# TensorE's order in a recurrence, a strip copy moved ahead of a root, and a closing stage in token halves

## The reference, cut to what matters

```
u = shift(h @ w_in)                              # "strips": u = keep*p + mu_prev*prev + mu_next*next
c_q, c_kv = c_q / rms(c_q), c_kv / rms(c_kv)     # the roots of the attention latents
S = S*w_t - (S kk_t) b_t + v_t k_t ; y_t = S r_t # 8 heads, forward and backward over the tokens
z = ALPHA*h + [y_att, y_rwkv] @ w_out
h = (z - mean(z)) / sqrt(var(z) + eps) * ln1_g + ln1_b
logits = h @ router
```

## Time and profile before

| | us |
|---|---|
| median of 3 runs (3505.91 to 3512.84) | 3507.08 |
| profiled execution, its own time | 3508.14 |
| its span, first to last instruction | 3505.9 |
| TensorE busy in the span | 3055.5 (87%) |
| VectorE, ScalarE, GpSimd busy | 1765.5, 843.7, 573.7 |
| mean granted TensorE clock | 0.933 |
| recurrence stage, layer 1 and 2 (first to last matmul) | 357.5 to 611.5, 1378.2 to 1632 |
| first y slot to the end of line 1787, layer 1 | 663.52 to 723.88 |
| the same, layer 2 | 1684.13 to 1742.29 |

### The profile page before, as it was taken

The page is one execution under the profiler, slowest core; times in us unless marked ns, Lnnn a source line. Parts: engine busy times, 40 slices in busy tenths (PEclk is TensorE's granted clock), DMA queues, the critical chain, the costliest instruction groups (busy, mean ns, idle before and its releaser), DMA issues. The chain is left out here.

```text
span 3505.9 us, 67363 instructions
## 1 busy us (share of the span) xinstructions
PE 3055.5 (87%) x27902; PEld 2335.8 (67%) x27902; DVE 1765.5 (50%) x3348; ACT 843.7 (24%) x1768; POOL 573.7 (16%) x895
## 2 busy tenths in 40 slices
PE   6899898958767997899868769899998899999998
PEld 4676788735436775887644434576656688778887
DVE  3445576441123444676421145255467776577742
ACT  3123222031122223222211132233354211122210
POOL 0000674011110003672011110000055200000000
PEclk9998799979988997899979979999999999999999
DMA  7110300269984102102199982101010122222220
GB/s 248 41 37 28 146 4 4 84 256 380 403 298 133 42 19 115 62 4 87 37 367 389 403 252 97 38 25 43 20 37 13 60 73 96 82 67 93 81 90 33
DMA packets 171506, 419.71 MB, mean 120 GB/s; under 512 B 30113, under 2 KB 116513, under 8 KB 145745
## 3 DMA queue, kind: packets, MB, share of 16 engines
q1 hardware_dynamic: 152241, 381.49, 29.2%
q0 software_dynamic: 8736, 17.32, 2.0%
q10 hardware_dynamic: 10240, 16.79, 1.5%
HBM read 398.82 MB, written 50.54 MB: 128 GB/s over the span
## 5 line engine op out<-in xcount | busy, mean ns | idle before, releaser
L2181 PE MATMUL ps<-e_w,e_xt 128*64 128x256 f32 x1792 | 231.0, 415 | 71.5 <-DMA e_w<-in_moe_w 70.1
L2181 PEld LDWEIGHTS ps<-e_w,e_xt 128*64 128x64 f32 x1792 | 151.8, 150 | 172.3 <-issue 84.1
L775 PE MATMUL ps<-h,win 128*128 128x264 f32 x960 | 229.5, 393 | 16.4 <-DVE pad L944 14.8
L2288 DVE TENSOR_TENSOR e_hid<-ps,e_silu 64x256 f32<-64x256 f32 x64 | 39.4, 615 | 399.8 <-ACT e_silu L2247 399.8
L775 PEld LDWEIGHTS ps<-h,win 128*128 128x128 f32 x960 | 182.8, 193 | 53.0 <-issue 22.0
L1462 PE MATMUL ps<-inv,nt 48*48 48x48 f32 x4224 | 133.6, 211 | 2.3 <-issue 2.3
L3712 PE MATMUL ps<-h_lat,wt 128*128 128x256 f32 x528 | 127.8, 384 | 6.7 <-ACT h_lat L3849 6.5
L3712 PE MATMUL ps<-h_lat,w_sums 128*128 128x256 f32 x544 | 130.8, 384 | 0.0
L2200 PE MATMUL ps<-e_w,e_hid_t 128*64 128x512 f32 x448 | 111.6, 617 | 12.6 <-DMA e_w<-in_moe_w 7.9
L1462 PEld LDWEIGHTS ps<-inv,nt 48*48 48x48 f32 x4224 | 116.9, 127 | 5.3 <-issue 2.6
L3712 PEld LDWEIGHTS ps<-h_lat,wt 128*128 128x128 f32 x528 | 101.1, 192 | 23.2 <-issue 7.3
(11 more groups left out here) (671 smaller groups left out, 6928.4 us busy)
## 6 DMA issues: line engine op xcount, KB each, us to landing
e_w<-in_moe_w SPq DMA_DIRECT2D x168, 1024.0 KB, 13.6
early<-in_moe_w SPq DMA_DIRECT2D x24, 1024.0 KB, 13.1
wt<-in_w_up SPq DMA_DIRECT2D x22, 1024.0 KB, 4.9
y_rows<-e_y ACTq DMA_DIRECT2D x128, 128.0 KB
win<-in_w_in SPq DMA_DIRECT2D x10, 1536.0 KB, 6.7
wmod<-in_w_mod SPq DMA_DIRECT2D x24, 512.0 KB, 15.1
wt<-in_w_in SPq DMA_DIRECT2D x11, 1024.0 KB, 4.8
early<-in_w_mod SPq DMA_DIRECT2D x16, 512.0 KB, 10.7
```

The source lines that it names most:

```text
L775: last = pe.matmul(ps[:, 7, 0:HT], lhsT=ring[(s + 1) % 2][:, i, o:o + P], rhs=k.h[:, i, h * HT:(h + 1) * HT], start=(i == 0), stop=(i == K ...
L2181: last = pe.matmul(ps[half, 2 + z, 0:EH], lhsT=xt[z][:, f, :], rhs=w[:, f, :], start=(f == 0), stop=(f == KD - 1))
L2288: dve.tensor_tensor(hid[z][high, :].rearrange("s (t q) -> s q t", t=2), ps[high, 2 + z, 0:EH].rearrange("s (q t) -> s q t", t=2), si[z][hi ...
```

## The change

TensorE alone takes the recurrence in another order: in a step, a chain that is at its last phase comes behind the others (11, 7, 3, 15). The other engines keep `woven()` as it was. In `mix_in` VectorE does `empty(1)` ahead of root 1 and `empty(2)` ahead of root 2. In `mix_close` the y slots come per half (eight y0 for columns 0 to 263, then eight y1), GpSimd adds the first six tiles of a half (`fold`), and mean, squares, root, reciprocal and router are done for half 0 between the y1 slots, for half 1 behind them.

```diff
+                    if t == 1:
+                        pe.wait_ge(root, 2)
...
                 empty(0)
+                empty(1)
                 for n in range(2):
...
-                    empty(n + 1)
+                    if n == 0:
+                        empty(2)
...
-        def woven():
+        def woven(last=None):
 
             for s in range(GAP * (CHAINS - 1) + STEPS):
                 for c in range(CHAINS):
-                    if 0 <= s - GAP * c < STEPS:
+                    if 0 <= s - GAP * c < STEPS and s - GAP * c != last:
                         yield c, s - GAP * c
+                for c in range(CHAINS):
+                    if last is not None and s - GAP * c == last:
+                        yield c, last
...
-                for c, p in woven():
+                for c, p in woven(last=STEPS - 1):
...
-                 + [("y", m) for m in range(KD)])
+                 + [("y0", m) for m in range(KD)] + [("y1", m) for m in range(KD)])
+        FOLD = 6
...
+                for h in range(2):
+                    hs = half_of(h)
+                    for m in range(1, FOLD):
+                        gp.wait_ge(emptied, at(f"y{h}", m) + 1)
+                        if m > 1:
+                            gp.wait_ge(ln_folded, (FOLD - 1) * h + m - 1)
+                        gp.tensor_tensor(fold[:, hs], k.h[:, 0, hs] if m == 1 else fold[:, hs], k.h[:, m, hs],
+                                         ALU.add).then_inc(ln_folded, 1)
...
+                def ln_mean(h):
+                    pe.wait_ge(ln_folded, (FOLD - 1) * (h + 1))
+                    pe.matmul(ps[:, 6 + h, 0:HT], lhsT=k.ones_d, rhs=fold[:, half_of(h)], start=True, stop=False)
+                    for m in range(FOLD, KD):
+                        pe.wait_ge(emptied, at(f"y{h}", m) + 1)
+                        last = pe.matmul(ps[:, 6 + h, 0:HT], lhsT=k.ones_d, rhs=k.h[:, m, half_of(h)],
+                                         start=False, stop=(m == KD - 1))
+                    last.then_inc(ln_summed, 1)
...
-                    if kind == "y" and n:
-                        ln_sum(n - 1)
-                ln_sum(KD - 1).then_inc(ln_summed, 1)
...
+                    if (kind, n) == ("y1", 0):
+                        ln_mean(0)
+                    elif (kind, n) == ("y1", 3):
+                        ln_spread(0)
+                    elif (kind, n) == ("y1", 6):
+                        route_half(0)
+                ln_mean(1)
+                ln_spread(1)
+                route_half(1)
...
+                empty("y1", 0)
+                mean(0)
+                centre(0, 0, 4)
+                empty("y1", 1)
+                centre(0, 4, KD)
+                empty("y1", 2)
+                empty("y1", 3)
+                invert(0)
+                scale(0, 0, 4)
+                empty("y1", 4)
+                scale(0, 4, KD)
+                for n in range(5, KD):
+                    empty("y1", n)
+                mean(1)
+                centre(1, 0, KD)
+                keep_logits(0)
+                invert(1)
+                scale(1, 0, KD)
+                keep_logits(1)
```

More of the change, by code:

```diff
@@ L1599, in mix_close @@
         st = sb("ln_st", [P, T])
+        fold = sb("ln_fold", [P, T])
         z2 = k.u[:, 0:KD, :]
@@ L1615, in two, with half_of @@
             return ps[:, 2 * (t % 3):2 * (t % 3) + 2, 0:HT]
+        def half_of(h):
+            return slice(h * HT, (h + 1) * HT)
         with k.stage("att_w0", "att_w1", "y_w", "sel_set", "spread_set", "pool_chain", "slot_made", "emptied", "gn_squared",
                      "gn_summed", "gn_rooted", "gn_inverted", "ln_summed", "ln_centred", "ln_squared", "ln_rooted",
-                     "ln_scaled", "logits_made", "logits_kept", "close_chain", "act_chain") as (
+                     "ln_scaled", "ln_folded", "logits_made", "logits_kept", "close_chain", "act_chain") as (
                 block, att_w0, att_w1, y_w, sel_set, spread_set, pool_steps, slot_made, emptied, gn_squared, gn_summed, gn_rooted,
-                gn_inverted, ln_summed, ln_centred, ln_squared, ln_rooted, ln_scaled, logits_made, logits_kept, steps,
-                act_steps):
+                gn_inverted, ln_summed, ln_centred, ln_squared, ln_rooted, ln_scaled, ln_folded, logits_made,
+                logits_kept, steps, act_steps):
             @block.sync
@@ L1650, in gn_sums, with ln_spread, route_half @@
                     last.then_inc(gn_summed, 1)
[L1652 to L1657, removed]
+                def ln_mean(h):
[6 more added lines that the diff above has]
+                    last.then_inc(ln_summed, 1)
+                def ln_spread(h):
+                    for i in range(KD):
+                        pe.wait_ge(ln_squared, KD * h + i + 1)
+                        last = pe.matmul(ps[:, 6 + h, 0:HT], lhsT=k.ones_d, rhs=z2[:, i, half_of(h)],
+                                         start=(i == 0), stop=(i == KD - 1))
+                    last.then_inc(ln_summed, 1)
+                def route_half(h):
+                    for f in range(KD):
+                        pe.wait_ge(act_steps, KD * h + f + 1)
+                        last = pe.matmul(ps[N_B * h:N_B * h + NR, 6 + h, 0:HT], lhsT=k.router[:, f, :],
+                                         rhs=k.h[:, f, half_of(h)], start=(f == 0), stop=(f == KD - 1))
+                    last.then_inc(logits_made, 1)
                 for t, (kind, n) in enumerate(slots):
@@ L1671, in _ @@
                         pe.wait_ge(spread_set, RT)
-                    if (kind, n) == ("y", 0):
+                    if (kind, n) == ("y0", 0):
                         pe.wait_ge(y_w, 16)
                         pe.wait_ge(emptied, at("gate", RT - 1) + 1)
-                    for h in range(2):
+                    for h in (int(kind[1]),) if kind in ("y0", "y1") else range(2):
                         hs, o = slice(h * HT, (h + 1) * HT), two(t)[:, h, :]
@@ L1715, in _ @@
                                scale=1.0 / N_B).then_inc(gn_rooted, 1)
[L1716 to L1724, removed]
+                for h in range(2):
+                    hs = half_of(h)
+                    for i in range(KD):
+                        act.wait_ge(ln_centred, KD * h + i + 1)
+                        act.activation(z2[:, i, hs], k.h[:, i, hs], ACT.Square).then_inc(ln_squared, 1)
+                    act.wait_ge(ln_summed, 2 * h + 2)
+                    act.activation(st[:, hs], ps[:, 6 + h, 0:HT], ACT.Sqrt, bias=k.eps("ln")).then_inc(ln_rooted, 1)
+                    for i in range(KD):
+                        act.wait_ge(ln_scaled, KD * h + i + 1)
+                        act.activation(k.h[:, i, hs], k.h[:, i, hs], ACT.Identity,
+                                       bias=k.par1[:, bias + i:bias + i + 1],
+                                       scale=k.par1[:, gain + i:gain + i + 1]).then_inc(act_steps, 1)
             @block.vector
@@ L1751, in empty, with centre, scale, mean @@
                     else:
-                        last = dve.tensor_tensor(split2(k.h[:, n, :]), split2(k.h[:, n, :]), o, ALU.add)
+                        h, hs = int(kind[1]), half_of(int(kind[1]))
+                        last = dve.tensor_tensor(k.h[:, n, hs], k.h[:, n, hs], o[:, h, :], ALU.add)
                     last.then_inc(emptied, 1)
+                def centre(h, lo, hi):
+                    hs = half_of(h)
+                    for i in range(lo, hi):
+                        dve.tensor_tensor(k.h[:, i, hs], k.h[:, i, hs], st[:, hs], ALU.subtract).then_inc(ln_centred, 1)
+                def scale(h, lo, hi):
+                    hs = half_of(h)
+                    dve.wait_ge(ln_centred, KD * (h + 1))
+                    for i in range(lo, hi):
+                        dve.tensor_tensor(k.h[:, i, hs], k.h[:, i, hs], st[:, hs], ALU.mult).then_inc(ln_scaled, 1)
+                def mean(h):
+                    dve.wait_ge(ln_summed, 2 * h + 1)
+                    chain(dve.tensor_copy(st[:, half_of(h)], ps[:, 6 + h, 0:HT]))
+                def invert(h):
+                    dve.wait_ge(ln_rooted, h + 1)
+                    chain(dve.reciprocal(st[:, half_of(h)], st[:, half_of(h)]))
+                def keep_logits(h):
+                    b = N_B * h
+                    dve.wait_ge(logits_made, h + 1)
+                    dve.tensor_scalar(k.logits_t[b:b + NR, :], ps[b:b + NR, 6 + h, 0:HT], k.router_b[b:b + NR, 0:1],
+                                      None, ALU.add).then_inc(logits_kept, 1)
                 def bonus_input(i):
@@ L1773, in _ @@
                 dve.reciprocal(root[:, :], root[:, :]).then_inc(gn_inverted, 1)
-                for kind, n in slots[at("att", 2):]:
+                for kind, n in slots[at("att", 2):at("y1", 0)]:
                     empty(kind, n)
[L1776 to L1788, removed]
+                empty("y1", 0)
[17 more added lines that the diff above has]
+                keep_logits(1)
 def early_place(k, n):
```

## The result

The changed kernel takes 3618.62 us (median of 4 runs, 3608.30 to 3628.76) against 3506.98 us (3505.91 to 3512.84): ratio 1.0315, interval 1.0278 to 1.0351. Forecast were 3583 us and 3520 to 3665. The profiled execution of the changed kernel took 3628.8 us, so it is the slowest of the four; its recurrence stages last 329.6 and 319.5 us where they lasted 254.0 and 253.9.

A forecast was written before the change was run, and what follows sets the result against it. A loop through TensorE and VectorE was taken to bound the recurrence. 3508.1 - 13.5 (strips) - 29 (closing stage) + 65 (order) + 53 (clock) = 3583.6, less 1.0: about 3583 us, range 3520 to 3665.

The forecast's parts named there:

- The loop and its term: In the recurrence, TensorE's phase 15 starts 1.70 us later per period, VectorE's list unchanged: 38 x 1.70 = 65 us slower.
- Rival (c): In the recurrence, moved phases use up today's wait: 0.32 us per period, 12 in all, 3477 us; chance 0.08.
- The clock: In the recurrence, new waits make TensorE's clock low for a quarter of the time: 53 us slower.
- Rival (a): In the recurrence, the clock stays at 2.4 GHz, so no 53 us: 3530 us; chance 0.22.
- Rival (b): In the recurrence, the clock is low two thirds of the time: 182 us in place of 53, 3712 us; chance 0.13.
- The strips: In `mix_in`, strip copies ahead of the root gain 6.8 us per layer, 13.5 in all, bounds 8 to 14.
- The closing stage: In `mix_close`, working in halves gains 15.7 us in layer one and 13.5 in layer two: 29 in all.
- Rival (d): In `mix_close`, the halves gain nothing since VectorE becomes late: 29 us more, 3612 us; no chance given.

The follow-up runs named there:

- the filled kernels: Changed kernel plus 8 or 3 useless matmuls per period behind phase 15 on TensorE: 3553.36 and 3552.56 us (ratios 1.0132 and 1.0128).
- the light kernel: Kernel with phase 15 last on both TensorE and VectorE, with GpSimd's four multiplies per chain cut to one eighth: 3481.24 us, ratio 0.9919.

## Why the prediction was right, and where its sizes were off

**The loop and its term.** Right. A phase 15 that starts 1.70 us later with VectorE's list unchanged gives 38 x 1.70 = 65 us; the filled kernels measure 67 by the medians, 62 by the periods, and a period of 11.69 us for 11.68. The waits came at 0.42 (0.56 said) and 2.03 us (2.0 said). Rival (c), that the moved phases only use up today's wait, is refuted by the same period.

**The clock.** The mechanism was right, the size was low: 53 us forecast, 65 measured. The weave's clock is 0.85 and 0.86 in the two layers, so TensorE is at 1.2 GHz for about 30% of the time and not for a quarter. Rival (a), 2.4 GHz throughout, gives 3530 us; it is what the filled kernels do, and the changed kernel doesn't. Rival (b), two thirds of the time low, overstated it. The Trainium skill (TensorE: Matmul & The Clock Gate, "HAM oscillation — how this bites in real kernels") puts falls down to gaps longer than any wait here; with 2.03 us, and again with 1.54 us in the kernel with TensorE's phase 15 third, the clock fell in most periods, so here the measurement decides against that rule. The same page's section "A second HAM failure mode: psum-queue depth-cycling" tells of a clock that oscillates from short, frequent idle times; these traces agree with that one. Relying on the one fall of the earlier trace rows was the better guide.

**The strips.** Right: 13.5 forecast, 13.1 measured by the medians and 13.0 by the traces; the wait of fill(3) was put at 1.9 and is 1.84.

**The closing stage.** This step failed: 29 us forecast, with bounds of 20 to 33; the trace of the changed kernel has 6.8 + 3.7 = 10.5, the part alone 10.3 by its traces and 12 by the medians. The prediction said "the squares' sum 8 x 0.22 = 1.78, the router the same". The 0.89 us of the earlier trace rows are one tile's sum over both halves, so a half is 0.445 and eight tiles are 3.56; I had halved twice. The rows show 3.72 and 3.75 for 16 instructions each. The mean has 6 instructions, 1.33 us, in place of 0.67. On TensorE this makes the last y1 slot end 37.4 us after the first instead of 32.7. The tail grows too: 16.2 us against 12.0 (708.2 - 696.2). The last copy and the mean take 0.5 us more than I had. The squares' sum ends 1.9 us behind the last subtraction, for 0.7. ScalarE's eight steps take 4.1 us for 3.6; I had called 0.45 a half of 0.73, and a step took 0.51. Router and logits end 2.6 us behind ScalarE's last step, for 0.9, at a clock of 0.74 (780.0 to 786.5 us). 4.7 + 4.1 is nearly the whole difference of 8.9 us in layer one. GpSimd's adds (0.74 us) stayed hidden. Rival (d) has the nearer number for this part, 0 against 29 for a measured 10.5, but not its cause: VectorE did not become late, and TensorE has no wait from the first y0 slot to the last y1 slot.

**The sum.** 3507 - 13.1 - 10.5 + 67 + 65 = 3615, for a measured 3618.6 (67 and 65 are differences of medians up to that very number, so their sum is no test of its own; the split between them is). The closing stage and the clock were off by 31 us together, in the same direction, and the range was wide enough for both.

## What to carry to other kernels

When engines that run in written order go through one loop together, a step moved on one of them has to be moved on the partner too. Against the old order on both, phase 15 last cost 132 us on TensorE alone and 9 on both engines; phase 15 third cost 105 on TensorE alone and brought 29 on both. So the place matters as well as the partner. Read from the timeline which instruction of the partner releases the next step, and count what stands ahead of it in the partner's list. Price a wait of TensorE twice, once as time and once as clock, and look for useful work to put into it; where there is none, even useless matmuls paid here, against the same order without them and not against the old order.

## What the runs showed of the hardware

A wait of 1.54 or 2.03 us in each period of a stream of small fp32 matmuls (10.7 or 11.7 us without a fall) took TensorE from 2.4 to 1.2 GHz, in 28 and 33 of 36 periods; waits of 0.82 us in a period of 9.98, 1.08 in 10.43 and 1.16 (with another of 0.42) in 11.69 left it at 2.4 GHz. The size of a wait alone doesn't decide: the single one of 1.84 us ahead of fill(3) left the clock at 1.00 (101.7 to 115 us of the changed kernel). A fall doesn't begin with the wait: the low clock mostly set in 0.4 to 1.9 us behind its end.

VectorE's COPY_PREDICATED 48x192 with both inputs in SBUF took 0.37 us in the median with no GpSimd instruction beside it and 0.66 beside one of GpSimd's TENSOR_TENSOR instructions (phase 15 last on both engines). The Trainium skill (SBUF — State Buffer, "SBUF: two separate sides") names a VectorE instruction with two SBUF inputs as one that needs the port pair it shares with GpSimd, against a GpSimd instruction that reads SBUF; the light kernel agrees, with 0.94 us for the pair instead of 1.40. The pair of copies from PSUM just ahead (L1575), with GpSimd's multiplies beside it, took 0.73 us in both kernels.
